# A decoder step: convolutions of the recurrence split in two, another signal for two banks, one sum moved

## The reference

```
xc = conv_b + sum(up[:, k:k + T] * conv_w[k] for k in range(4))
r = sigmoid(xb @ w_rg_a + b_rg_a)          # per block
i = sigmoid(xb @ w_rg_i + b_rg_i)
log_a = -8 * r * softplus(-lru_lambda);  a = exp(log_a)
b = sqrt(-expm1(2 * log_a)) * (i * xc)
h[t] = a[t] * h[t-1] + b[t]
y = h * gelu(u_gate)
merged = sigmoid(g_a) * (o_attn @ w_branch_attn) + sigmoid(g_b) * (y @ w_branch_rnn)
```

## Time and profile before

| | |
|---|---|
| median of 3 runs | 2303.85 us (2299.04 to 2308.78) |
| the profiled execution | 2302.16 us |
| its span, first to last instruction | 2300.3 us |
| mean granted TensorE clock | 0.983 |
| TensorE busy | 2189.7 us, 95% |
| VectorE busy | 962.0 us, 42% |
| ScalarE busy | 650.8 us, 28% |
| instructions | 28827 |

### The profile page before, as it was taken

One profiled execution on the slowest core, in us unless ns is written; L12 is line 12 of the kernel. 1 busy time (PEld: TensorE's weight loads), 2 busy tenths in 40 slices (PEclk: granted clock), 3 DMA queues, 4 the chain that ended last, 5 costly groups with the idle time before them and its releaser, 6 DMA issues.

```text
span 2300.3 us, 28827 instructions
## 1 busy us (share of the span) xinstructions
PE 2189.7 (95%) x10100; PEld 1397.5 (61%) x10100; DVE 962.0 (42%) x2069; ACT 650.8 (28%) x1375; POOL 455.1 (20%) x890
## 2 busy tenths in 40 slices
PE   8998999999999998999998999899999999999985
PEld 6455665667677777888885556445454545445442
DVE  0226888844366665344443567511111111111116
ACT  3125666644435543011111220011111111111112
POOL 0002444300100000000000000134443434343430
PEclk9998999999999999999999999999999999999997
DMA  6302000154421111112213114599999999999945
GB/s 210 112 7 95 2 2 1 61 196 171 181 63 30 37 37 39 28 50 88 74 37 117 55 57 164 192 353 351 346 351 337 346 343 348 352 341 340 340 101 221
DMA packets 133214, 378.25 MB, mean 164 GB/s; under 512 B 23891, under 2 KB 81355, under 8 KB 105835
## 3 DMA queue, kind: packets, MB, share of 16 engines
q1 hardware_dynamic: 109587, 292.46, 34.4%
q0 software_dynamic: 23520, 84.36, 12.8%
HBM read 341.48 MB, written 58.00 MB: 174 GB/s over the span
## 4 chain that ended last, share of the span: by engine, by line
PE 84%; DVE 8%; ACT 3%; DMA 2%; issue 2%; SPq 0%; POOL 0%; DVEq 0%; ACTq 0%; POOLq 0%
PE PS L1438 19%; PE PS L1226 19%; PE PS L1449 10%; PE PS L761 8%; PE PS L874 5%; PE PS L1351 4%; PE PS L907 3%; PE PS L944 3%; PE PS L1335 2%; PE PS L1044 2%; PE PS L809 1%; PE PS L1390 1%; PE PS L1173 1%; ACT arena L1527 1%; DVE arena L2249 1%
## 5 line engine op out<-in xcount | busy, mean ns | idle before, releaser
L1226 PE MATMUL PS<-arena 128*128 128x258 f32 x2352 | 517.2, 382 | 11.4 <-issue 3.5
L1226 PEld LDWEIGHTS PS<-arena 128*128 128x128 f32 x2352 | 447.1, 191 | 80.6 <-issue 5.6
L1527 ACT ACTIVATE arena<-PS 128x512 f32<-128x512 f32 (+9 forms) x602 | 275.9, 470 | 744.3 <-PE PS L761 413.2
L1438 PE MATMUL PS<-arena 128*128 128x512 f32 x1040 | 457.2, 592 | 0.8 <-ACT arena L1527 0.8
L761 PEld LDWEIGHTS PS<-arena 128*128 128x128 f32 (+3 forms) x1950 | 234.5, 159 | 194.3 <-issue 128.8
L1438 PEld LDWEIGHTS PS<-arena 128*128 128x128 f32 x1040 | 192.9, 190 | 218.6 <-issue 217.6
L761 PE MATMUL PS<-arena 128*128 128x128 f32 (+3 forms) x1950 | 286.2, 278 | 37.7 <-DVE arena L2059 8.1
L1449 PE MATMUL PS<-arena 128*128 128x512 f32 x520 | 239.2, 593 | 0.5 <-ACT arena L1527 0.5
L2539 DVE TENSOR_TENSOR arena<-PS,arena 128x256 f32<-128x256 f32 x65 | 27.6, 425 | 432.2 <-ACT arena L1867 432.2
L2652 POOL MEMSET arena<- 128x2 f32 x1 | 0.1, 99 | 773.1 <-PE PS L1351 773.1
L1449 PEld LDWEIGHTS PS<-arena 128*128 128x128 f32 x520 | 94.0, 191 | 93.9 <-issue 93.3
(11 more groups left out here) (336 smaller groups left out, 2214.6 us busy)
## 6 DMA issues: line engine op xcount, KB each, us to landing
arena<-in_w_exp_gate SPq DMA_DIRECT2D x65, 1024.0 KB
arena<-in_w_exp_up SPq DMA_DIRECT2D x65, 1024.0 KB
arena<-in_w_exp_down SPq DMA_DIRECT2D x65, 1024.0 KB
arena<-in_w_in SPq DMA_DIRECT2D x34, 512.0 KB, 4.9
arena<-in_x_prompt SPq DMA_DIRECT2D x16, 512.0 KB, 3.7
expert_rows<-arena SPq DMA_DIRECT2D x16, 512.0 KB
arena<-expert_rows SPq DMA_DIRECT2D x6, 1024.0 KB, 11.7
arena<-in_w_in SPq DMA_DIRECT2D x16, 256.0 KB, 8.0
```

Source lines behind the costliest of these rows:

```text
L1226: ins = mm(PS[:, bank, 0:QT], lhs[:, l0 + k, :], right[:, r0 + k, c0:c0 + QT], start=first and k == 0, stop=k == kh - 1, skip_group_check= ...
L1438: ins = mm(PS[:, 2 + s, :].rearrange("p (h n) -> p h n", h=2), xgT[:, s, k, :], up_w[w][:, :, k, :], start=k == 0, stop=k == KT - 1)
L1527: return fn(out, in_, ACT.Copy)
```

## The change

`CONV` is replaced by `CONV_A` and `CONV_B`, and `conv` by `conv_first` and `conv_second`. The first part makes those columns of `xc` that need only the first half pair of the input block: 0 to 257 and, but for the first three, 516 to 773. The second makes the rest and the sample tokens, and signals `xc_done`. The first parts of channels 1 to 7 stand at u = 1, 5, 9 and 11, the second at u = 2, 6, 10 and 12, all ahead of `first_add`. On ScalarE the r sigmoid waits for a new count of `dp_ready`, signalled by the product with the root in `recur`; the wait for `hs_done` moves behind it, to the i sigmoid. In the last half pair of the "ux" stage (u = 13), `right_first("wb")` is made ahead of `first_add`, and `recur_rows` and `gate_rows(7)` ahead of `last_adds`. `gated_input` becomes a `step`.

```diff
@@ -518,7 +518,8 @@
         PAIRS = [(2 + 2 * i, ("ux" if i < 7 else "wb" if i < 11 else "wa" if i < 15 else "gx")) for i in range(23)]
         YB, YA, GX = 7, 11, 15
         AFTER = {0: 0, 2: 1, 3: 2, 6: 3, 7: 4, 10: 5, 11: 6, 12: 7}
-        CONV = {2: (1, 2), 6: (3, 4), 10: (5, 6), 12: (7,)}
+        CONV_A = {1: (1, 2), 5: (3, 4), 9: (5, 6), 11: (7,)}
+        CONV_B = {2: (1, 2), 6: (3, 4), 10: (5, 6), 12: (7,)}
         GELU = {2: slice(1, 3), 3: slice(1, 3), 6: slice(0, 2), 7: slice(0, 2), 10: slice(1, 2), 11: slice(1, 2), 12: slice(0, 3, 2), 13: slice(0, 3, 2)}
         GG_AT = {0: 0, 1: 1, 2: 2, 3: 0, 4: 1, 7: 1, 5: 2, 6: 0}
         G_EV = {0: 1, 1: 3, 2: 3, 3: 5, 4: 5, 7: 7, 5: 9, 6: 9}
@@ -1777,9 +1778,11 @@
                     if n is not None:
                         act.wait_ge(sem("r_mm"), n + 1)
                         if n:
-                            act.wait_ge(sem("hs_done"), n)
+                            act.wait_ge(sem("dp_ready"), 6 + n)
                         E.do(fn(rr.rearrange("p (a b) -> p a b", a=4), PS[:, bank:bank + 4, 0:QT], ACT.Sigmoid, bias=vec[:, n, 37:38]), sem("r_ev"))
                         act.wait_ge(sem("i_mm"), n + 1)
+                        if n:
+                            act.wait_ge(sem("hs_done"), n)
                         E.do(fn(ii.rearrange("p (a b) -> p a b", a=4), PS[:, 4 - bank:8 - bank, 0:QT], ACT.Sigmoid, bias=vec[:, n, 38:39]), sem("i_ev"))
                     act.wait_ge(st_mm, PROD * u + 1)
                     if j == 0 and i in (0, 2, 4):
@@ -2234,25 +2237,39 @@
                     src = PS[GP[g], 6, 0:2 * P].rearrange("p (s q r) -> p r s q", s=2, q=4)[:, 4 * g:4 * g + 4, :, :]
                     E.step(V.tensor_copy(AT[GP[g], :, SEQ:NTOK].rearrange("p j (s q) -> p j s q", s=2), src), sem("win_read") if g else None)
 
-            def conv(n):
-
-                E.step(V.tensor_copy(ucs[:, :, 0:3], vec[:, n, 0:24].rearrange("p (b r) -> p b r", b=BD)))
-                if n == 0:
-                    dve.wait_ge(sem("u_ev"), 1)
-                elif n >= 2:
+            def conv_first(n):
+
+                if n >= 2:
                     dve.wait_ge(sem("i_mm"), n - 1)
                 cw = lambda k: vec[:, n, 32 + k:33 + k]
+                halves = lambda x, k: x[:, k:k + NTOK].rearrange("p (t c) -> p t c", t=2)[:, :, 3:QT]
                 src, dst = ucb[:, n % 2, :], xc[:, n % 2, :]
-                E.do(ts(dst[:, 0:SEQ], src[:, 0:SEQ], cw(0), vec[:, n, 36:37], ALU.mult, ALU.add))
-                E.step(ts(dst[:, SEQ:NTOK], ucs[:, :, 0], cw(0), vec[:, n, 36:37], ALU.mult, ALU.add))
+                E.do(ts(dst[:, 0:3], src[:, 0:3], cw(0), vec[:, n, 36:37], ALU.mult, ALU.add))
+                E.step(ts(halves(dst, 0), halves(src, 0), cw(0), vec[:, n, 36:37], ALU.mult, ALU.add))
                 for k in range(1, 4):
-                    E.do(stt(dst[:, 0:SEQ], src[:, k:k + SEQ], cw(k), dst[:, 0:SEQ], ALU.mult, ALU.add))
-                    E.step(stt(dst[:, SEQ:NTOK], ucs[:, :, k] if k < 3 else src[:, 1027:1035], cw(k), dst[:, SEQ:NTOK], ALU.mult, ALU.add))
+                    E.do(stt(dst[:, 0:3], src[:, k:k + 3], cw(k), dst[:, 0:3], ALU.mult, ALU.add))
+                    E.step(stt(halves(dst, 0), halves(src, k), cw(k), halves(dst, 0), ALU.mult, ALU.add))
+
+            def conv_second(n):
+
+                cw = lambda k: vec[:, n, 32 + k:33 + k]
+                src, dst = ucb[:, n % 2, :], xc[:, n % 2, :]
+                E.step(V.tensor_copy(ucs[:, :, 0:3], vec[:, n, 0:24].rearrange("p (b r) -> p b r", b=BD)))
+                for k in range(4):
+                    for c0, c1 in ((QT, HT + 3), (HT + QT, SEQ)):
+                        if k == 0:
+                            E.do(ts(dst[:, c0:c1], src[:, c0:c1], cw(0), vec[:, n, 36:37], ALU.mult, ALU.add))
+                        else:
+                            E.do(stt(dst[:, c0:c1], src[:, c0 + k:c1 + k], cw(k), dst[:, c0:c1], ALU.mult, ALU.add))
+                    if k == 0:
+                        E.step(ts(dst[:, SEQ:NTOK], ucs[:, :, 0], cw(0), vec[:, n, 36:37], ALU.mult, ALU.add))
+                    else:
+                        E.step(stt(dst[:, SEQ:NTOK], ucs[:, :, k] if k < 3 else src[:, 1027:1035], cw(k), dst[:, SEQ:NTOK], ALU.mult, ALU.add))
                 E.step(V.tensor_copy(stg[:, n, 0:11], src[:, 1024:1035]), sem("xc_done"))
 
             def gated_input(n):
                 dve.wait_ge(sem("i_ev"), n + 1)
-                E.do(tt(ii, ii, xc[:, n % 2, :], ALU.mult))
+                E.step(tt(ii, ii, xc[:, n % 2, :], ALU.mult))
 
             def norm_input(n):
                 dve.wait_ge(sem("a_done"), n + 1)
@@ -2260,7 +2277,7 @@
 
             def recur(n):
                 dve.wait_ge(sem("sq_done"), n + 1)
-                E.step(tt(ii, ii, rr, ALU.mult))
+                E.step(tt(ii, ii, rr, ALU.mult), sem("dp_ready"))
                 E.do(V.tensor_tensor_scan(RT[:, n, 0:SEQ], aa[:, 0:SEQ], ii[:, 0:SEQ], 0.0, ALU.mult, ALU.add))
 
             def recur_rows(n):
@@ -2335,7 +2352,9 @@
                 E.step(tt(yb, yb, gb, ALU.mult))
                 E.step(tt(yb, yb, ya, ALU.add), sem("mg_done"))
 
-            conv(0)
+            dve.wait_ge(sem("u_ev"), 1)
+            conv_first(0)
+            conv_second(0)
             left_sums(0)
             decode_out()
             dve.wait_ge(w_used, 2)
@@ -2344,28 +2363,31 @@
             for i in range(YB):
                 for j in range(2):
                     u = 2 * i + j
-                    n, turns = AFTER.get(u - 1), CONV.get(u, ())
+                    n = AFTER.get(u - 1)
                     if n is not None:
                         gated_input(n)
-                    if turns:
-                        conv(turns[0])
+                    for c in CONV_A.get(u, ()):
+                        conv_first(c)
+                    for c in CONV_B.get(u, ()):
+                        conv_second(c)
+                    if u == 2 * YB - 1:
+                        right_first("wb")
                     first_add(i, j)
                     if n is not None:
                         norm_input(n)
                     mid_add(i, j)
                     if n is not None:
                         recur(n)
-                    if len(turns) > 1:
-                        conv(turns[1])
+                    if u == 2 * YB - 1:
+                        recur_rows(n)
+                        gate_rows(n)
                     last_adds(i, j)
-                    if n is not None:
+                    if n is not None and n != KT - 1:
                         recur_rows(n)
                     if j == 0:
                         left_sums(i + 1)
                     for g in GATED.get(u, ()):
                         gate_rows(g)
-            right_first("wb")
-            gate_rows(7)
             gate_rows(5)
             gate_rows(6)
             right_rest("wb")
```

## The result

The changed kernel takes 2308.9 us, the median of 20 runs (2306.1 to 2314.6), against 2300.2 before, run alongside it (20 runs). The ratio is 1.0036, 95% interval 1.0029 to 1.0043: 8.3 us slower, 6.7 to 9.9. The forecast was 7.4 us. So a difference well under the 11.5 us that the prediction took for the least that can be told shows here, since each kernel ran 20 times. The profiled execution took 2311.67 us, its span 2309.7. Lines behind L519 have moved: the products are now L1227, the i product L1291, `mid_add` L2337, the last add L2348, `gate_rows` L2290.

What follows compares the result with a forecast made beforehand. Only about 22 us of TensorE standing still in the recurrence stage can be touched. +2.4 - 3 x 1.34 - 1.75 + 2 x 4.4 - 1.4 = +4.0, with the clock +7.4: 2311 us forecast, range 2303 to 2318.

Steps and rivals of the forecast that it cites:

- Price of the split: VectorE's convolution as first part 3.55 us and second part 4.6, together 8.1 against 5.85, twelve more instructions per channel.
- Half pairs 1 and 2: P7 of u = 2 waits 4.7 us for the mid add, the i product's 3.13 us wait goes: +2.4 us.
- Half pairs 5, 6, 9 and 10: P7 of u = 5 and 9 waits 5.8 us, the i products' 2.24 us wait goes: +4.4 us, twice.
- The banks' signal: P1 stops waiting: -1.34 us at u = 4, 8 and 12, and -1.75 together at u = 12 and 13.
- The last half pair: At u = 14 P2 waits no more and P3 still waits about 4.5 us: -1.4 us.
- The clock: Lower-clock spells behind TensorE waits go from two to four at 1.7 us each: +3.4 us.
- the clock stays up: Rival: the new TensorE waits bring no further slow spell, +0.6 to +5 us, some 2307 us; chance 0.20.
- Longer slow spells: Rival: each of the four TensorE waits is followed by about 3.4 us lost, +14, 2318 us; chance 0.13.
- First parts in idle time of VectorE: Rival: P7 of u = 2, 5 and 9 is not held, 16 us saved, 2287 us; chance 0.05.
- The banks' signal frees nothing: Rival: something else holds ScalarE or P1, the gains of 1.34 and 1.2 vanish, +12.6, 2316 us; chance 0.07.

Runs made afterwards that it cites:

- The split alone: Kernel before with only the convolutions in two parts, the two other edits undone: ratio 1.0058 against before, 13.3 us slower.
- the waits filled: Changed kernel plus 9, 12 and 12 matmuls nobody reads in front of P7 of u = 2, 5 and 9: ratio 1.0007 against before.
- the last experiment: Whole convolutions, second ones behind the last adds, both other edits, plus 9 unread matmuls before P3 of u = 14: ratio 0.9922 against before.
- the banks' signal alone: Kernel before with only the r sigmoid's new signal and the hs_done wait moved to the i sigmoid: ratio 0.9984 against before, 3.7 us faster.
- without the split: Kernel before with the banks' signal and last half pair edits, convolutions whole where they were: ratio 0.9966 against before, 7.8 us faster.
- the first parts behind the mid add: Changed kernel with the first parts at u = 5 and 9 moved from ahead of the first add to behind the mid add: ratio 1.0025 against before.

## Why the prediction was right, and where a term was off

- *Price of the split.* 3.53 + 4.55 us measured, 3.55 + 4.6 in the sum. The twelve added instructions and their handovers cost 2.2 us a channel (8.08 less 5.85). The rule of the Trainium skill ("VectorE: DVE Perf Modes", section on the TRN2 errata) that each instruction on SBUF operands pays a fixed part agrees in kind with this; an estimate from its 151 cycles makes 1.9.
- *Half pairs 1 and 2.* A wait of 4.57 us was measured where 4.7 was forecast, and the i product lost its 3.13. The split alone shows the same. Two things in the prediction's working are hard to follow. Its terms, added as they are listed, make 28.85; its 27.6 comes out only if the 2.35 already holds the 1.22 of normalising, and so it is in the trace (684.93 to 687.29 in the changed kernel). And a P7 that starts at 703.9 instead of 698.11 would wait 6.2 us, not 4.7, if nothing held TensorE before; the 4.7 needs a wait of some 1.5 at P7 of u = 1, which the prediction does not name and of which 1.32 was measured. The +2.4 does not depend on that: in the changed kernel it is 4.1 from P7 of u = 0 to the i product of u = 2, less the 1.7 of the clock.
- *Half pairs 5, 6, 9 and 10.* 5.64 and 5.97 us where 5.8 was forecast. The sum also had 0.9 us of waiting for P7 of u = 6 and 10. That did not come: P1 to P6 of u = 6 ran in part at the lower clock, and P7 was late by itself. With the waits filled it comes back, 0.74 and 0.75 us. So the prediction counted these 1.8 us in the queue's term, though the slow stretch, which has a term of its own, uses up the same time.
- *The banks' signal.* 1.34 us at each of three places, as forecast, 4.9 in all for the edit alone. In the changed kernel u = 12 waits its 0.56, as forecast, since S(7) is shorter.
- *The last half pair.* P3 of u = 14 waits 4.31 us (4.5 forecast), and 1.4 us are won up to there. In the changed kernel they stay won; in some executions of the other kernels the stretch behind P3 took up to 1.1 of them back.
- *The clock.* This term was mis-sized. Forecast were two spells more at 1.7, +3.4 us. Measured in the changed kernel: P7 of u = 2, 3.50 us to the r product instead of 1.81, so 1.7; from P7 of u = 5 to the next r product 17.05 instead of 14.0, so 3.0; the same at u = 9 with 16.78, so 2.8; and 1.9 behind P3 of u = 14, 9.4 together. Before it was 1.7 at 826 and 1.9 behind P3, 3.6. So +5.8. (The 1.9 behind P3 is in both, and by the last experiment it cost neither kernel anything, since P7 would have waited; the prediction counted it as 1.7 lost, on both sides.) The three stretches behind the waits of P7 were then taken away with the matmuls that fill them, which gave 5.7 us; 7.5, less the 1.5 of P7's waits that come back, would be 6.0.

Summed anew: +4.0 less the 1.8 of the two waits that did not come, +5.8 of clock, 8.0 against 7.9 in the stage. The mechanism was right: VectorE's queue, the places of the waits and the lower clock behind them. That the total fits to 1 us is in part luck, two errors of opposite sign, +1.8 and -2.4.

Of the rivals, "the clock stays up" is refuted by the windows at 0.50 and by the filled waits. "Longer slow spells" was half true: 3.0 and 2.8 us behind the two longest waits, 1.7 and 1.9 behind the two shorter, where it had 3.4 behind each. "First parts in idle time of VectorE" holds for u = 11 alone, where P7 does not wait, and moving them behind the mid add did not find room in u = 5. That no other place there would have had room follows from the length of VectorE's queue; no run tried one. "The banks' signal frees nothing" is refuted by its own experiment.

Open: why one wait of 2.24 us is followed by the lower clock and its twin is not. In the kernel before it was the one at u = 10, with the banks' signal alone the one at u = 6, and without the split the one at u = 10 again, and besides it the wait of 3.13 at u = 2, which in the kernel before drew nothing. These are single executions.

## What to carry to other kernels

Moving work to an earlier place in an engine's written-out order costs nothing only if it fits between the row in front of it and the deadline of the row behind it; here 7.1 us were put in front of an add that had some 1.2 to spare. Moving whole convolutions behind the last adds, into idle time that the timeline showed, made the waits go that splitting them was meant to shorten. Splitting an instruction pays its fixed part again, here 0.19 us for each of the twelve added ones, so try moving whole pieces first. And price a wait of TensorE twice: once for its length, once for the lower clock behind it, unless the work behind it would have waited anyway. How long the stretch will be could not be told beforehand here.

## What the runs showed of the hardware

- Each unfilled wait of more than 4 us was followed by a stretch at the 1.2 GHz level, and what it cost is not settled by the wait's length: behind waits of 4.3 to 4.7 us TensorE took 1.4 to 3.1 us longer (P7 of u = 2 with the split alone, 3.24 us to the r product instead of 1.81; P7 of u = 6 with the first parts behind the mid add, 6.60 us to the i product instead of 3.55), behind waits of 5.6 to 6.0 us 2.3 to 3.0 (with the split alone, 14.62 us for the 56 instructions at u = 5 instead of 12.34; in the changed kernel, 17.05 instead of 14.0). Waits of 2.2 and 3.1 us drew it in some executions and not in others.
- Matmuls whose results nobody reads, put into waits of 4.3 to 6.0 us, kept the granted clock at 1.00, the 2.4 GHz level, behind each of the four waits filled, and no cost of theirs was found: P7 started no later behind P7 of the half pair before than without them (16.9 and 17.0 us at u = 2).
